# A hybrid attention block on one core: the first attention block prepared inside the last weight tile, and VectorE's sort and mask work in pieces

## The chip, the cores and the metric

One core of one Trainium2 chip. The metric is the device time of one execution in microseconds. The profile is one execution recorded by the hardware profiler; its times are counted from the start of its span.

## The reference

One layer, x of 2048 tokens by 1024, fp32:

```python
proj = x @ w_in                      # qa ka va ga | qi ki wi | qb kb vb gb
# group A: every query keeps the 256 best visible keys, 8 heads, one key/value head
score = sum_h w_h * relu(qi_h . ki)  # visible: key chunk <= query chunk (chunks of 64)
idx   = top_k(score, 256)
ya    = softmax(qa . ka[idx] / 8 - slope * |t - idx|) @ va[idx]
# group B: window of two chunks, 8 heads on 2 key/value heads, a sink per head
yb    = softmax([qb . kb / 8 - slope * dist, sink])[..., :-1] @ vb
y     = concat(ya * silu(ga), yb * silu(gb)) @ w_out
out   = layer_norm(2 ** 0.25 * x + y) * g + b
```

## The kernel before

**The projection.** The weights are 20 tiles of 128 columns, the tokens two halves of 1024. For each half, TensorE takes tile by tile; a `product` is the six matmuls of one of the 8 row blocks k of a tile (`product`, L1345; values are split into a high and a low part, three products each, two banks of 512). ScalarE takes the tile out of the PSUM (`evacuate`) and stores it to `proj` in DRAM. Sixteen groups `norm(b)` of 24 matmuls (L1363) make values and indexer weights in natural layout, into bank 4 or 6; ScalarE takes them out (`leave_norm`).

**The search.** Queries are dealt with in blocks of 128, two blocks to a pair; the pairs come in the order 0, 1, 2, 3, 7, 6, 5, 4, and `p` counts along it (so p = 4 is the longest, with 2048 keys, p = 5 has 1792, p = 6 1536, p = 7 1280). For pair p TensorE makes `dots` (L1377), ScalarE `relu` (L1208), VectorE `sum` (L1580); dots(p, j, c, w, h) is query block j, keys from c, w of them, heads h and h+1, in bank 4 + h for p up to 5. Then VectorE turns the scores into sortable integers (`sortable`, L1596: sign bits, flip, mask to the upper half), and 32 steps of bisection find the level of the 256th key: `search` on VectorE for one block of the pair, `sign` on ScalarE for the other, and for p of 5 and above GpSimd decides (`decide_own`, `decide_sign`). At the end come `limits`, `equal`, and `masks` (L1667): two scans that rank equal keys, one operation that marks those taken, two that write the mask, in one piece.

**The attention.** Blocks b = 0 to 15 follow the same order. For each: the band (`load_qb`, `round_qb`, `split_qb`, `window`, `bias_b`, `exp_b`, `level_b`, `turn_b`, `mix_b`, `gate_b`), the scan for the row maxima (`scan` on TensorE, two banks; `scan_max`, L1733, on VectorE; `turn_max`, `leave_max`, L1757; `place_max`, a DMA), and the units `logits`, `exp_a`, `values` over the key tiles, then `turn_a`, `y_a`, `columns_a`, `gate_a`. From block 12 on, the probabilities are split and `low_a` (VectorE for one half, GpSimd for the other) makes their low part. The scan of block b+1 needs the maximum of block b (L1423). The units of block b need its mask from DRAM for b of 2 and above.

**The hand-over.** Late buffers lie in the memory of early ones. So the first loads wait for the last matmul of the projection: `load_qa(0)`, `load_bias`, `shift_values`, `extra_rows` (constant rows of `qa_ext`, and `upper`), the memsets of `setup_pieces` (L1704, VectorE). `load_keys_a` (L815) puts the raw keys into the buffer of `relu` and waits until the last sum of pair 5 is done; ScalarE rounds them (`round_keys_a`), GpSimd subtracts (`split_keys_a`). The first scan needs all of these.

**The order.** No order is written by hand. `whole_plan` lists pieces with an engine, a cost and what they need; a list scheduler places them, and its ranks are shifted by a table of numbers, `PREFER`, one for each kind of piece. Every engine and DMA queue then runs its pieces in that order.

```python

pe.wait_ge(a_left_max, b)      # scan of block b, L1423
sp.wait_ge(summed, 4 * chunks_before(NPAIR - 2))   # load_keys_a, L817
```

Of the kernel before, what the change touches and what calls it, by code (L numbers as in the profile page):

```python
# [23 lines left out]
F32 = mybir.dt.float32  # L24
# [16 lines left out]
H = 8  # L41
# [31 lines left out]
            "keys_rest", "load_wo")  # L73


def index_chunks(p):


    n = 2 * P * (PAIRS[p] + 1)
    chunks = [(j, c, min(512, n - c)) for j in range(2) for c in range(0, n, 512)]  # L80
    return sorted(chunks, key=lambda chunk: p == NPAIR // 2 and chunk[1] >= HALF)


FAMILY = {"index": ("load_index", "queries", "split_index", "dots", "relu", "sum"),
          "search": ("sortable", "begin", "search", "sign", "turn", "limits", "equal", "above", "masks"),
          "band": ("load_qb", "round_qb", "split_qb", "window", "bias_b", "max_b", "exp_b", "put_sink", "den_b", "level_b", "turn_b",
                   "copy_b", "mix_b", "gate_b"),
          "scan": ("load_qa", "round_qa", "split_qa", "positions", "scan", "scan_max", "top_of_chunks", "turn_max", "leave_max", "place_max"),
          "units": ("logits", "exp_a", "low_a", "values", "leave_a"),
          "tail": ("turn_a", "y_a", "columns_a", "gate_a")}  # L90
# [93 lines left out]
def whole_plan():  # L184
# [6 lines left out]
    def dots_of(p, bank_lock):  # L191
# [5 lines left out]
        for p, j, c, w, h in parts:  # L197
# [7 lines left out]
            add("DVE", 0.25 + 1.05 * w / 512, "sum", *part,  # L205
                needs=[("relu", *part), ("leave_norm", BLOCKS[2 * p + j]), sums[-1], ("masks", p - 1)])
            sums.append(("sum", *part))
        add("DVE", 0.6 + 5.1 * n / 1000, "sortable", p, needs=[sums[-1]])
        add("DVE", 0.15, "begin", p, needs=[("sortable", p), ("store_masks", p - 1)])
        for i in range(32):  # L210
            if i == 16:
# [37 lines left out]
    def products(half, t, k):  # L249
# [1661 lines left out]
```

## Time and profile before

| | us |
|---|---|
| median of 3 runs | 1454.12 (1453.76 to 1454.82) |
| the profiled execution | 1462.23 |
| its span | 1460.4 |
| TensorE busy | 1359.3 (93%) |
| VectorE busy | 1130.6 (77%) |
| ScalarE busy | 896.8 (61%) |
| GpSimd busy | 629.6 (43%) |

The profiled execution is 8.1 us longer than the median. Busy time is that of instructions; register, semaphore and DMA-issuing instructions are not counted. The granted clock of TensorE is given as a share of 2.4 GHz: 1.00, or 0.50 (1.2 GHz), or a mean over a stretch. A row of a timeline has start, duration, engine, line, operation, output <- inputs and, in brackets, the idle time before it with what ended it. Matmuls overlap, so that the distance between two starts is what one costs.

### The profile page before, as it was taken

How to read it: one execution, taken by the hardware profiler on the slowest of the kernel's cores; microseconds unless marked ns; L12 is line 12 of the kernel's file. 1: busy time of each engine (PE TensorE's matmuls, PEld its weight loads, DVE VectorE, ACT ScalarE, POOL GpSimd, SP SyncE). 2: the span in 40 equal slices, each digit the busy share in tenths (PEclk: the TensorE clock that was granted, in tenths of full speed). 3: DMA queues.
4: the chain of work that ended last, by engine and by line, in shares of the span. 5: the costliest groups of instructions: out<-in, count | busy, mean ns of one | idle time of the engine just before them, and what ended most of it. 6: DMA issues, size and time to landing. Idle time of an engine off the chain costs nothing. (4 is left out here: it accounts for less than half of the span.)

```text
span 1460.4 us, 18810 instructions
## 1 busy us (share of the span) xinstructions
PE 1359.3 (93%) x6006; PEld 993.5 (68%) x6052; DVE 1130.6 (77%) x2215; ACT 896.8 (61%) x1687; POOL 629.6 (43%) x726
## 2 busy tenths in 40 slices
PE   7999999899999995798999799999999799999997
PEld 5888887698888874565655456655555565588886
DVE  3486879864899887778889999889898967257675
ACT  3395885873498736777775488885678676700010
POOL 2421332633422336466544256534336577423332
PEclk9999999999999996699999999999999899999999
DMA  7412232325232328233433132402011143134442
GB/s 241 127 60 80 87 105 80 117 91 154 73 109 94 101 90 174 66 89 87 113 92 88 45 83 56 104 21 64 27 28 26 39 133 118 44 122 146 144 148 83
DMA packets 106548, 136.85 MB, mean 94 GB/s; under 512 B 6643, under 2 KB 83383, under 8 KB 106191
## 3 DMA queue, kind: packets, MB, share of 16 engines
q1 hardware_dynamic: 93296, 93.23, 23.4%
q10 hardware_dynamic: 9504, 31.66, 5.5%
q0 software_dynamic: 3648, 10.76, 2.5%
q8 instruction: 48, 0.79, 0.2%
q14 instruction: 52, 0.42, 0.1%
HBM read 92.20 MB, written 42.34 MB: 92 GB/s over the span
## 5 line engine op out<-in xcount | busy, mean ns | idle before, releaser
L1644 DVE TENSOR_SCALAR_CACHE_REDUCE above<-dist,trial 128x512 bf16<-128x512 int32 (+13 forms) x224 | 345.9, 1544 | 28.9 <-POOL trial L1002 23.9
L1179 ACT ACTIVATE above<-dist,trial 128x384 bf16<-128x384 int32 (+13 forms) x224 | 280.8, 1254 | 60.8 <-DVE trial L1617 24.3
L1356 PE MATMUL psum<-x_hi,w_hi 128*128 128x512 f32 x640 | 251.8, 393 | 16.0 <-DVE x_lo L1693 10.6
L1356 PE MATMUL psum<-x_lo,w_hi 128*128 128x512 f32 x640 | 250.8, 392 | 0.0
L1356 PE MATMUL psum<-x_hi,w_lo 128*128 128x512 f32 x640 | 250.5, 391 | 0.0
L1290 ACT ACTIVATE prob<-psum 128x512 f32<-128x512 f32 x272 | 159.8, 593 | 115.8 <-PE psum L1506 54.6
L1748 DVE CUSTOM_DVE_ANT_0 junk<-psum,mask 128x512 bf16<-128x512 f32 (+3 forms) x320 | 184.4, 605 | 26.7 <-PE psum L1430 16.1
L1506 PE MATMUL psum<-prob,vw 128*65 128x512 f32 x376 | 184.8, 597 | 0.1
L1493 PE MATMUL psum<-qa_mix,ka_mix 128*128 128x512 f32 x272 | 162.4, 597 | 5.5 <-DMA qa_ext<-minus_max 3.7
L1430 PE MATMUL psum<-ka_ext,qa_ext 128*128 128x512 f32 (+3 forms) x320 | 134.1, 467 | 27.4 <-ACT ka_mix L1129 12.3
L941 POOL CAST w_hi<-raw 128x1024 fp32r<-128x1024 f32 x40 | 49.7, 1243 | 253.1 <-PE psum L1356 248.8
L1356 PEld LDWEIGHTS psum<-x_hi,w_hi 128*128 128x128 f32 x640 | 121.1, 189 | 43.2 <-issue 11.1
L1356 PEld LDWEIGHTS psum<-x_hi,w_lo 128*128 128x128 f32 x640 | 121.1, 189 | 25.6
L1356 PEld LDWEIGHTS psum<-x_lo,w_hi 128*128 128x128 f32 x640 | 121.2, 189 | 24.9
L1215 ACT ACTIVATE relu<-psum 128x1024 f32<-128x1024 f32 (+1 forms) x76 | 71.4, 957 | 86.2 <-PE psum L1389 54.2
L1593 DVE SCALAR_TENSOR_TENSOR score<-relu,vw,score 128x512 f32<-128x512 f32 (+1 forms) x114 | 101.5, 891 | 12.3 <-ACT relu L1215 5.9
L1494 PE MATMUL psum<-qa_ext,ka_ext 128*128 128x512 f32 x272 | 109.2, 402 | 0.0
L1430 PEld LDWEIGHTS psum<-ka_ext,qa_ext 128*128 128x128 f32 x320 | 63.0, 201 | 66.9 <-issue 32.1
L1129 ACT ACTIVATE yt_hi<-yt_raw 128x1024 fp32r<-128x1024 f32 x16 | 17.0, 1061 | 140.2 <-PE psum L1555 126.7
L949 POOL TENSOR_TENSOR w_lo<-raw,w_hi 128x1024 fp32r<-128x1024 f32 x38 | 100.0, 2632 | 5.8 <-POOL w_hi L941 0.4
L1555 PE MATMUL psum<-wo_hi,yt_hi 128*128 128x512 f32 x256 | 99.8, 390 | 0.1
L1555 PE MATMUL psum<-wo_hi,yt_lo 128*128 128x512 f32 x256 | 99.6, 389 | 0.0
(161 smaller groups left out, 2906.8 us busy)
## 6 DMA issues: line engine op xcount, KB each, us to landing
raw<-w_tiles SPq DMA_DIRECT2D x40, 512.0 KB, 3.7
proj<-staged ACTq DMA_DIRECT2D x40, 512.0 KB, 3.3
qb_raw<-proj SPq DMA_DIRECT2D x32, 256.0 KB, 4.0
qa_raw<-proj SPq DMA_DIRECT2D x32, 256.0 KB, 4.5
yt_raw<-y_t SPq DMA_DIRECT2D x16, 512.0 KB, 5.1
x_row<-x_res SPq DMA_DIRECT2D x16, 512.0 KB, 3.9
out<-z ACTq DMA_DIRECT2D x16, 512.0 KB, 2.6
x_raw<-xT SPq DMA_DIRECT2D x12, 512.0 KB, 4.2
```

What stands on the lines that cost most here:

```text
L949: nc.gpsimd.tensor_tensor(w_lo[:, u, :, :].rearrange("p k c -> p (k c)"), raw[:, u, :], w_hi[:, u, :, :].bitcast(F32).rearrange("p k c -> ...
L1179: nc.scalar.activation(above[:, 0, 0:n], src, ACT.Sign, scale=-1.0, bias=u, accum_out=count[:, 0:1]).then_inc(sign_counted, 1)
L1290: last = nc.scalar.activation(prob[:, unit % 3, :], psum[:, 4 + unit % 2, :], ACT.Exp, scale=0.125)
L1356: last = pe.matmul(psum[:, 2 * u + m, :], wt[:, u, k, :], xt[:, k, 512 * m:512 * m + 512], start=(k == 0 and q == 0), stop=(k == KT - 1 an ...
L1430: last = pe.matmul(psum[:, bank, 0:w], qa_ext[:, s, h, :], ka_ext[:, s, c:c + w], start=True, stop=not diag)
L1493: pe.matmul(o, ka_mix[:, ks], flat(qa_mix[:, s, hs, :]), start=False, stop=False)
L1494: last = pe.matmul(o, ka_ext[:, s, ks], flat(qa_ext[:, s, hs, :]), start=False, stop=(kt < BLOCKS[b]))
L1506: pe.matmul(psum[0:65, 6 + g, :], vw[:, kt, 0:65], prob[:, u % 3, :], start=(kt == 0), stop=(kt == BLOCKS[b])).then_inc(a_used, 1)
L1555: last = pe.matmul(psum[:, 4 + 2 * s + m, :], yt[:, s, k, :], wt[:, k, cols], start=(k == 0 and q == 0), stop=(k == KT - 1 and q == 2))
L1593: v.scalar_tensor_tensor(o, relu[:, h, 0:w], wt, o, ALU.mult, ALU.add).then_inc(summed, 1)
L1644: v.tensor_scalar(above[:, 1, 0:n], src, u, None, ALU.is_ge, ALU.add, accum_out=count[:, 1:2]).then_inc(own_counted, 1)
L1748: v.tensor_tensor_reduce(out=junk[:, scan % 2, 0:w], in0=psum[:, scan % 2, 0:w], in1=mask[:, s, c:c + w], scale=1.0, scalar=-3.0e38, op0=A ...
```

## The change

1. The raw keys go into the memory of `values_hi` and `values_lo` instead of `relu`, so their load no longer waits for the sums of pair 5; `split_values` now waits until the keys are taken.
2. The loads and constants of the first block wait for single products of tile 19 (`last_tile(k)`), not for its end. Buffers are placed anew to allow that: `qa_raw` moves to the front, `yt_a` and `gate_a` behind `y_a`.
3. The memsets of the start leave VectorE (`setup_pieces` is gone) and become seven on GpSimd (`fill`).
4. `sortable` is cut into `sign_bits`, `flip`, `sortable`; `masks` into `rank` (twice), `taken`, `masks`. The operations are the same; other work of VectorE may now stand between the pieces.
5. norm(9) need only stand before tile 19; the plan's costs of `decide_own` and `decide_sign` go from 0.45 to 0.53; the whole of `PREFER` is new, so that many pieces change places.

```diff
+FILLS = 7
-PREFER = {'above': -36689.1, 'band0': -163507.6, ...
+PREFER = {'above': -221597.0, 'band0': -79525.8, ...
-        add("DVE", 0.6 + 5.1 * n / 1000, "sortable", p, needs=[sums[-1]])
+        add("DVE", 0.6 + 1.7 * n / 1000, "sign_bits", p, needs=[sums[-1]])
+        add("DVE", 0.1 + 2.1 * n / 1000, "flip", p, needs=[("sign_bits", p)])
+        add("DVE", 0.1 + 1.3 * n / 1000, "sortable", p, needs=[("flip", p)])
-        add("DVE", 0.9 + n * 0.0077, "masks", p, needs=[("equal", p), ("above", p)])
+        add("DVE", 0.3 + n * 0.0024, "rank", p, 0, needs=[("equal", p), ("above", p)])
+        add("DVE", 0.1 + n * 0.0024, "rank", p, 1, needs=[("rank", p, 0)])
+        add("DVE", 0.2 + n * 0.0022, "taken", p, needs=[("rank", p, 1)])
+        add("DVE", 0.3 + n * 0.0011, "masks", p, needs=[("taken", p)])
...
+        if (half, t) == (1, N_TILES - 1) and k == 0:
+            needs.append(("norm", NORM_ORDER[-1]))
...
-        keys_a_raw = flat(relu)
+        keys_a_raw = [values_hi[:, :, :].bitcast(F32).rearrange("p b n -> p (b n)")[:, 0:HALF],
+                      values_lo[:, :, :].bitcast(F32).rearrange("p b n -> p (b n)")]
+
+        def last_tile(k):
+
+            return (x_used, KT + k) if k < KT - 1 else (tile_mm, 2 * N_TILES)
...
             def load_keys_a():
                 sp.wait_ge(stored[0], 16 * (N_TILES // 2 + 2))
-                sp.wait_ge(summed, 4 * chunks_before(NPAIR - 2))
...
             def load_bias():
-                sp.wait_ge(tile_mm, 2 * N_TILES)
+                sp.wait_ge(*last_tile(1))
...
             def extra_rows():
-                pool.wait_ge(tile_mm, 2 * N_TILES)
+                pool.wait_ge(*last_tile(4))
...
-                settled()
-                nc.gpsimd.memset(row_top[:, :], 0.0).then_inc(setup_pool, 1)
-                latest[0] = (setup_pool, 2)
+            def fill(top):
+
+                pieces = [(2, mask[:, 0, 0:P], 0.0), (2, mask[:, 1, 0:2 * P], 0.0), (2, mask[0:HD, 0, HD:P], -BIG),
+                          (2, mask[0:HD, 1, P + HD:2 * P], -BIG), (2, lb[:, :, 0:HD], 0.0), (5, vs[0:HD, 0, :], 0.0),
+                          (KT - 1, row_top[:, :], 0.0)]
+                for i in ((FILLS - 1,) if top else range(FILLS - 1)):
+                    k, where, value = pieces[i]
+                    pool.wait_ge(*last_tile(k))
+                    settled()
+                    nc.gpsimd.memset(where, value).then_inc(filled, 1)
+                    latest[0] = (filled, i + 1)
...
             def split_values(i):
                 if i == 0:
                     pool.wait_ge(norm_out, NB)
+                    pool.wait_ge(keys_taken, 2)
...
-                if n_dots == 2 * chunks_before(NPAIR - 2):
-                    act.wait_ge(keys_lo, 2)
...
-                elif (half, t) == (0, N_TILES - 1):
+                elif t == N_TILES - 1:
                     last.then_inc(x_used, 1)
...
-                for j in range(2):
-                    last = v.tensor_tensor_scan(rank[:, j, 0:n], equal[:, j, 0:n], equal[:, j, 0:n],
-                                                n_above[:, j:j + 1], ALU.add, ALU.max)
-                step(last)
+                step(v.tensor_tensor_scan(rank[:, j, 0:n], equal[:, j, 0:n], equal[:, j, 0:n],
+                                          n_above[:, j:j + 1], ALU.add, ALU.max))
```

The order on TensorE in tile 18 of the second half. Lines 1356 (before) and 1379 (now) are products, 1387 and 1389 (now 1410 and 1412) dots of pair 5, 1395 norm(9). Before, from dots (5, 0, 512) for heads 2 and 3 on:

```order
L1387 MATMUL psum<-ki_hi,qi_split 128x512
L1389 MATMUL psum<-ki_lo,qi_split 128x512
L1387 MATMUL psum<-ki_hi,qi_split 128x512
L1389 MATMUL psum<-ki_lo,qi_split 128x512
L1356 MATMUL psum<-x_hi,w_hi 128x512
L1356 MATMUL psum<-x_lo,w_hi 128x512
L1356 MATMUL psum<-x_hi,w_lo 128x512
L1356 MATMUL psum<-x_hi,w_hi 128x512
L1356 MATMUL psum<-x_lo,w_hi 128x512
L1356 MATMUL psum<-x_hi,w_lo 128x512
L1387 MATMUL psum<-ki_hi,qi_split 128x512
L1389 MATMUL psum<-ki_lo,qi_split 128x512
```

Now, from the same dots on:

```order
L1410 MATMUL psum<-ki_hi,qi_split 128x512
L1412 MATMUL psum<-ki_lo,qi_split 128x512
L1410 MATMUL psum<-ki_hi,qi_split 128x512
L1412 MATMUL psum<-ki_lo,qi_split 128x512
L1379 MATMUL psum<-x_hi,w_hi 128x512
L1379 MATMUL psum<-x_lo,w_hi 128x512
L1379 MATMUL psum<-x_hi,w_lo 128x512
L1379 MATMUL psum<-x_hi,w_hi 128x512
L1379 MATMUL psum<-x_lo,w_hi 128x512
L1379 MATMUL psum<-x_hi,w_lo 128x512
L1395 MATMUL psum<-wn_hi,x_hi 128x196
L1395 MATMUL psum<-wn_lo,x_hi 128x196
```

The norm, 24 matmuls of which two are shown, moved from the start of the second half to this place. In tile 19 five groups of dots of pair 5 stand now where there were seven, the last two narrow, and the other groups come behind its last product, around the two window groups.

The order on GpSimd around the end of the projection, from the band's first split on. Before:

```order
L1020 TENSOR_TENSOR kb_lo<-kb_raw,kb_hi 128x2x128
L1024 TENSOR_TENSOR qb_mix<-qb_raw,qb_mix 64x2x256 x2
L964 TENSOR_TENSOR qi_split<-qi_raw,qi_split 64x1024
L988 DMA qa_ext<-c_extm 64x1024 x2
L989 DMA upper<-c_upper 128x256
L991 MEMSET row_top 128x128
L981 TENSOR_TENSOR ka_mix<-relu,ka_ext 64x1024
L1067 MEMSET qa_ext 1x1024
```

Now:

```order
L1043 TENSOR_TENSOR kb_lo<-kb_raw,kb_hi 128x2x128
L1047 TENSOR_TENSOR qb_mix<-qb_raw,qb_mix 64x2x256 x2
L1002 DMA qa_ext<-c_extm 64x1024 x2
L1003 DMA upper<-c_upper 128x256
L1014 MEMSET mask 128x128
L1014 MEMSET mask 128x256
L1014 MEMSET mask 64x64 x2
L1014 MEMSET lb 128x8x64
L1014 MEMSET vs 64x128
L1014 MEMSET row_top 128x128
L1091 MEMSET qa_ext 1x1024
L1098 TENSOR_TENSOR qa_mix<-qa_raw,qa_mix 64x1024
```

The split of the indexer's queries for pair 6 moved behind, the splits of the keys stand ahead of this piece, and the fills are new.

The order on VectorE around the masks of pair 5 (p = 5). `minus_max` is `leave_max` of block 7. Before:

```order
L1755 TENSOR_REDUCE row_top<-part_max 128x8
L1761 TENSOR_SCALAR minus_max<-psum 8x128
L1672 TENSOR_SCALAR n_above<-n_above 128x2
L1674 SCALAR_TENSOR_TENSOR score<-score,n_above 128x1792 x2
L1677 SCALAR_TENSOR_TENSOR dist<-score,dist 128x2x1792
L1680 TENSOR_SCALAR above<-dist,trial 128x1792 x2
```

Now:

```order
L1700 SCALAR_TENSOR_TENSOR score<-score,n_above 128x1792
L1822 RECIPROCAL rec_a<-psum 128x8
L1826 TENSOR_TENSOR y_a<-psum,rec_a 128x512
L1769 ISA junk,part_max<-psum,mask 128x512
L1769 ISA part_max 128x1
L1776 TENSOR_REDUCE row_top<-part_max 128x8
L1705 SCALAR_TENSOR_TENSOR dist<-score,dist 128x2x1792
L1808 TENSOR_TENSOR yt_a<-psum,gate_a 128x512
L1711 TENSOR_SCALAR above<-dist,trial 128x1792 x2
L1782 TENSOR_SCALAR minus_max<-psum 8x128
```

The maximum of block 7 stood ahead of the whole mask work and stands behind it now. For pair 5's start, VectorE did all sums, the sort and the first search step ahead of the first band operation; now the last sums and the sort pieces stand between the reductions of blocks 0 and 1, and four search steps come before the second maximum instead of eight. Around the sort of pair 6, sign bits and flip stand ahead of the last reduction of block 8, and y_a of block 7 comes three search steps later instead of right behind the sort. Around the masks of pair 7, `low_a` pieces of block 13 stand ahead of the first scan and between scans and `taken`.

## Rows read from the trace of the kernel before

**Rows 1.** Windows: stretch, its length, busy PE, PEld, DVE, ACT, POOL (instructions), clock, DMA, GB/s
```profile
526.00:536.00 10.00, 7.77 (x29) 6.36 (x30) 7.78 (x13) 4.70 (x5) 0.00 (x0) 0.83 0.47 157
560.00:600.00 40.00, 18.57 (x64) 13.56 (x66) 28.24 (x73) 31.64 (x51) 26.64 (x40) 0.59 0.77 154
760.00:800.00 40.00, 37.16 (x150) 20.83 (x152) 37.23 (x64) 24.61 (x51) 16.95 (x9) 1.00 0.35 88
820.00:850.00 30.00, 17.65 (x75) 12.83 (x75) 29.01 (x64) 17.53 (x35) 11.27 (x22) 0.77 0.25 71
1140.00:1170.00 30.00, 22.56 (x93) 14.76 (x93) 28.62 (x54) 18.59 (x32) 16.03 (x22) 0.78 0.20 58
```

**Rows 2.** Timeline of TensorE, end of the projection: start, duration, what, [idle before]
```profile
555.30 0.39 PE L1356 MATMUL psum<-x_hi,w_lo 128*128 128x512 f32 x1
...
572.14 0.44 PE L1430 MATMUL psum<-ka_ext,qa_ext 128*128 128x128 f32 x1 [12.28 <-ACT ka_mix L1129]
...
584.63 0.99 PE L1493 MATMUL psum<-qa_mix,ka_mix 128*128 128x512 f32 x1 [2.97 <-DMA qa_ext<-minus_max]
```

**Rows 3.** Timelines of SyncE and GpSimd there, and two DMA issues with landing time
```profile
539.37 0.58 SPq L810 DMA_DIRECT2D qb_raw<-proj  x1
...
548.52 2.73 POOL L1024 TENSOR_TENSOR qb_mix<-qb_raw,qb_mix 64x512 fp32r<-64x512 f32 x2
557.54 2.56 POOL L988 DMA_DIRECT2D qa_ext<-c_extm  x2
571.05 0.94 POOL L1067 MEMSET qa_ext<- 1x1024 f32 x1 [3.39 <-DMA upper<-c_upper]
...
power<-c_pow POOLq DMA_DIRECT2D x1, 512.0 KB, 5.1
upper<-c_upper POOLq DMA_DIRECT2D x1, 128.0 KB, 10.9
```

**Rows 4.** Tile 18: timelines of TensorE and ScalarE; and line 1372 in 320 to 420
```profile
520.27 0.39 PE L1387 MATMUL psum<-ki_hi,qi_split 128*128 128x512 f32 x1
522.54 0.39 PE L1387 MATMUL psum<-ki_hi,qi_split 128*128 128x512 f32 x1
528.23 0.47 PE L1387 MATMUL psum<-ki_hi,qi_split 128*128 128x512 f32 x1 [3.27 <-ACT relu L1215]
...
528.74 1.02 ACT L1215 ACTIVATE relu<-psum 128x1024 f32<-128x1024 f32 x1 [0.65 <-DVE score L1593]
...
320.00:420.00 100.00, 7.25 (x65) 7.07 (x64) 1.00 0.39 116
```

**Rows 5.** Timeline of VectorE behind the sums of pair 5
```profile
555.82 3.66 DVE L1607 TENSOR_SCALAR dist<-score 128x3584 int32<-128x3584 int32 x1
559.51 3.89 DVE L1608 TENSOR_TENSOR score<-score,dist 128x3584 int32<-128x3584 int32 x1
563.44 2.03 DVE L1609 TENSOR_SCALAR dist<-score 128x3584 int32<-128x3584 int32 x1
...
566.93 2.08 DVE L1644 TENSOR_SCALAR_CACHE_REDUCE above<-dist,trial 128x1792 bf16<-128x1792 int32 x1
...
581.69 0.28 DVE L1761 TENSOR_SCALAR minus_max<-psum 8x128 fp32r<-8x128 f32 x1 [1.73 <-PE psum L1455]
...
602.27 0.27 DVE L1761 TENSOR_SCALAR minus_max<-psum 8x128 fp32r<-8x128 f32 x1
```

**Rows 6.** Timeline of VectorE, mask work of pair 5
```profile
773.81 4.51 DVE L1677 SCALAR_TENSOR_TENSOR dist<-score,dist 128x3584 f32<-128x3584 int16 x1
778.35 4.13 DVE L1680 TENSOR_SCALAR above<-dist,trial 128x1792 bf16<-128x1792 f32 x2
```

**Rows 7.** Timeline of TensorE behind the sort of pair 6
```profile
832.10 1.09 PE L1531 MATMUL psum<-ident,y_a 128*128 128x128 f32 x4 [6.21 <-DVE y_a L1805]
```

**Rows 8.** Timeline of VectorE, two equal operations of the sums
```profile
539.08 0.49 DVE L1590 TENSOR_SCALAR score<-relu,vw 128x512 f32<-128x512 f32 x1 [0.37 <-ACT relu L1215]
548.64 1.45 DVE L1590 TENSOR_SCALAR score<-relu,vw 128x512 f32<-128x512 f32 x1 [1.22 <-ACT relu L1215]
```

More of the change, by code:

```diff
@@ L84 @@
 FAMILY = {"index": ("load_index", "queries", "split_index", "dots", "relu", "sum"),
-          "search": ("sortable", "begin", "search", "sign", "turn", "limits", "equal", "above", "masks"),
+          "search": ("sign_bits", "flip", "sortable", "rank", "taken", "begin", "search", "sign", "turn", "limits", "equal", "above", "masks"),
           "band": ("load_qb", "round_qb", "split_qb", "window", "bias_b", "max_b", "exp_b", "put_sink", "den_b", "level_b", "turn_b",
@@ L298, in whole_plan @@
             tile(half, t)
-            if (half, t) == (0, N_TILES - 1):
-                for b in NORM_ORDER[0:8]:
+            if t == N_TILES - 1:
+                for b in NORM_ORDER[8 * half:8 * half + 8]:
                     norm(b)
@@ L303, in whole_plan @@
                 products(half, t, k)
-        if half:
-            for b in NORM_ORDER[8:]:
-                norm(b)
         for p in ((1, 2, 3), (4, 5))[half]:
@@ L312, in whole_plan @@
         add("POOL", 1.0, "keys_rest", i, needs=[("norm", NORM_ORDER[-1]), ("split_x2", 2 * KT + 1), ("round_keys", 1)])
[L313 removed]
+    last = lambda k: ("product", 1, N_TILES - 1, k)
+    add("SP", 1.4, "load_keys_a", needs=[("store", 1, 2)])
     for i in range(2):
[L315 removed]
+        add("ACT", 3.2, "round_keys_a", i, needs=[("load_keys_a",), ("split_x2", 2 * KT + 1), ("norm", NORM_ORDER[-1])])
         add("POOL", 2.6, "split_keys_a", i, needs=[("round_keys_a", i)])
     add("POOL", 1.0, "load_power", needs=[("split_w", 1, N_TILES - 1)])
[L318 to L319 removed]
+    add("SP", 0.4, "load_bias", needs=[last(1)])
+    add("POOL", 3.2, "extra_rows", needs=[last(4), ("load_power",)])
     add("ACT", 1.0, "setup_act", needs=[end])
[L321 to L324 removed]
+    for i in range(2):
+        add("POOL", 0.35 if i else 2.2, "fill", i, needs=[end if i else last(5), ("fill", i - 1)])
+    add("ACT", 0.25, "put_sink", 0, needs=[("fill", 0)])
+    add("SP", 3.6, "shift_values", needs=[last(5), ("leave_norm", NORM_ORDER[-1])])
     stores = [("store", 1, N_TILES - 1), ("store", 1, N_TILES - 2)]
@@ L368, in whole_plan @@
         add("SP", 0.4, "place_max", b, needs=[("leave_max", b), ("positions", b)])
-        add("PE", 0.9, "turn_b", b, holds="banks2", until=("copy_b", b), needs=[("level_b", b), ("setup_dve",), ("mix_b", b - 1)])
+        add("PE", 0.9, "turn_b", b, holds="banks2", until=("copy_b", b), needs=[("level_b", b), ("fill", 0), ("mix_b", b - 1)])
         add("ACT", 1.03, "copy_b", b, needs=[("turn_b", b), ("mix_b", b - 1)])
@@ L1741, in scan_max @@
                 if scan == 0:
-                    for i in range(2):
-                        dve.wait_ge(stored[i], 16 * N_TILES)
+                    dve.wait_ge(stored[0], 16 * N_TILES)
+                    dve.wait_ge(tile_mm, 2 * N_TILES)
+                    dve.wait_ge(filled, FILLS)
                 dve.wait_ge(a_scan, scan + 1)
```

113 lines of the change are left out of this document (54 added, 59 removed).

## The prediction

> **What bounds the kernel now.** I read the busy time and the granted clock by stretches first, and of each row the busy time of TensorE, that of VectorE and the clock. From 560 to 600 us, just behind the projection, TensorE is busy 18.57 of 40 us at a mean clock of 0.59, the worst stretch of the kernel. Two smaller dips lie at 820 to 850 (17.65 of 30, clock 0.77) and 1140 to 1170 (22.56 of 30, 0.78), and in both VectorE is full, 29.01 and 28.62 of 30. An ordinary stretch, 760 to 800, has TensorE busy 37.16 and VectorE 37.23 of 40 [rows 1]. So both engines are close to being the bound, and time is lost where TensorE waits for something that the start of the attention or VectorE owes it.
>
> The timeline of TensorE shows the hand-over: the last product starts at 555.30 and ends at 555.7, the first scan comes at 572.14 behind 12.28 us of idle time, the first logits at 584.63 [rows 2]. The queues of GpSimd and SyncE and the landing times show what was late: GpSimd issued the constant rows only from 557.54, because they waited for the end of the projection; the last one, `upper`, took 10.9 us to land and released the memset at 571.05; `power`, on the same queue at a quieter time, took 5.1 [rows 3].
>
> **Step 1: a matmul group that moves.** norm(9), the last of the natural-layout products, goes from the start of the second half into tile 18, behind two groups of dots of pair 5. 65 such matmuls are busy 7.25 us, so its 24 take 2.7 [rows 4], and TensorE reaches tile 18 that much earlier. But norm(9) writes bank 6, which the dots just ahead of it fill. The ReLU that empties the bank ran from 528.74 for 1.02 us, to 529.8, since it waits for sums that stand behind the mask work of pair 4 on VectorE, which does not move. Before, a dots group (4 matmuls) and a product (6 matmuls of the same size) together took 522.54 - 520.27 = 2.27, so 0.91 and 1.36 [rows 4]. Now the two dots groups, and the product between them and norm(9), end at 520.27 - 2.7 + 1.36 + 2 x 0.91 + 1.36 = 522.1. Then TensorE waits until 529.8, 7.7 us where 3.27 stood [rows 4]: **+4.4 us** on the end of the projection. The ends are 0, if VectorE finishes the masks of pair 4 sooner, and +6, if the longer wait doubles the clock loss of the stretch behind it, which was 10 x 0.17 = 1.7 us between 526 and 536 [rows 1].
>
> **Step 2: the hand-over.** From 529.8, norm 2.7, two dots groups 1.8, four products 5.4 and the clock loss of 1.7 end tile 18 at 541.4. Tile 19 has eight products (10.9) and now 3.7 of dots, so the projection ends at 556.0; another 3.7 us of dots that used to lie inside it come behind. The band's loads are issued at the end of tile 18. Before, they were issued from 539.37, and GpSimd's split of the queries ended at 548.52 + 2.73 = 551.25, 11.9 later [rows 3]; that gives 553.3 now. The constant rows come right behind it. Their issue took 2.56 plus 0.6 for `upper`, so they are out at 556.4, and `upper` lands between 561 (with 5.1) and 567 (with 10.9). The fills that left VectorE run on GpSimd meanwhile. VectorE had 1.46 us for them and `begin` between 563.44 + 2.03 and 566.93 [rows 5]; on GpSimd the flight of `upper` covers them, and without that cover I would charge 2. The keys' six copies on ScalarE, 1.02 each by the ReLU of the same size [rows 4], lie in tiles 18 and 19, beside dots which VectorE paces.
>
> VectorE is late by its own account. Of pair 5, the sums of (1,512) and (1,1024) and the eight band operations now stand ahead of its first reduction, and each dots group needs its ReLU and sums before a buffer is free. Behind 556.0 come a dots group, a ReLU (1.02), and two and a half double groups of sums at 4 x 0.5 to 4 x 0.9, which with about 2 of band work reach 566 to 567. I take the first scan at **567, 5 us earlier** than 572.14; the ends are 562 (all as early as the quick landing allows) and 572 (nothing gained).
>
> From there to the first maximum (`leave_max`) it took 9.6 us, 572.14 to 581.69, with a search step of 2.08 inside. That span now also holds 2.0 of sums (four at 0.49 [rows 8]), 3.66 of sign bits and 3.89 of flipping [rows 5], and no search step: 9.6 if these fall into VectorE's waits, 17 if all waits stay. With 12.5 the maximum comes at 579.5 and the logits 2 us earlier than before. Up to the second maximum VectorE owes 2.03 of sorting, four search steps and eight reductions; that is 595 instead of 602.27, with four steps (8.3 us) fewer done [rows 5]. TensorE is 7 us ahead and VectorE's total work 1 behind. As neither engine alone is the bound [rows 1], I take **-3 us, step 1 included**, between -7 and +1.
>
> A rule speaks against giving GpSimd more to do. An operation that takes VectorE 0.49 at 539.08 took 1.45 at 548.64 [rows 8], beside GpSimd's subtraction that began at 548.52 [rows 3]. I keep to that excess, 1 us for each of three subtractions that run beside sums and sort pieces, and the -3 holds it. The Trainium skill (SBUF — State Buffer, "Who interferes with whom") makes it a lock: a VectorE operation with two SBUF inputs or in a two-port mode and a GpSimd one that reads SBUF exclude each other for a whole instruction. By that rule the trace agrees; what it would do here in full is the third rival.
>
> **Step 3: the parts.** Cutting adds one semaphore wait between the two scans of a pair; I cost it at nothing, against scans of several us. What counts is what now stands between the pieces.
> - Pair 6, at 820 to 850. TensorE waits 6.21 us for y_a, which stands behind the whole sort [rows 7]; it is idle 12.4 in all [rows 1]. Now four key tiles of block 7 stand beside sign bits and flip, and only the last sort piece, a search step and gate_b stand before the maximum: -5.
> - Pair 7, at 1140 to 1170, 7.4 idle [rows 1]. Low halves of block 13 now stand between mask pieces, but the two scans stay together: -3.
> - Pair 5, the other way round. Before, the maximum of block 7 came ahead of the mask work, and TensorE ran block 7 beside it, busy 37.16 of 40 from 760 to 800 [rows 1]. Now `taken` (4.51) and `masks` (4.13) [rows 6] and gate_a (about 0.7) stand ahead of that maximum, and TensorE's next work, the scan of block 8, needs it: 9.3 us idle. The units it would have done are not lost; they fill its holes up to 850. I charge 5.
>
> Sum of step 3: **-3 us**, between -9 and +6.
>
> **Sum.** -3 - 3 = -6 us. The profiled execution took 1462.23 us with a span of 1460.4, 8.1 above the median of the runs; the terms are differences inside it, so I take them from the median, 1454.1: **1448 us**.
>
> **Rivals.**
>
> *The maximum behind the masks (slower).* If block 7's units find no hole later, all 9.3 us stay, and the clock falls as it did at 820 to 850: 30 x 0.23 = 7 us of clock there for 12.4 of idle time, so 5 for 9.3. With +1 for the hand-over and -8 for the other two places that is +7: 1461; with -3 for the hand-over 1457. I put 1459. It decides when more than 8 us of the wait and its clock stay. For it: no such wait exists there now. Against: VectorE is full behind it, so TensorE has holes anyway. Chance 0.21.
>
> *VectorE is the bound (no change).* The search of pair 5 starts four steps late, each pair starts when the one before is done, and TensorE's 7 us become idle time before the masks. The same comes out if `upper` lands late and the change does not bring the first scan forward. +1 for the hand-over and -1 for the parts: 1454. For it: VectorE is busy 28.24 of 40 in the gap itself, so there is not much to win for it. Chance 0.15.
>
> *GpSimd's reads stop VectorE.* Three subtractions of 2.73 [rows 3] delay VectorE by 8.2 instead of the 3 in the sum, so -6 becomes -1: 1453. One operation in the rows was held for 1 us, none for 2.7. Chance 0.07.
>
> *Both gains in full.* TensorE's 7 us carry to the end and the parts give back 8: 1439. For it: TensorE is 93% busy there, so a lead counts. Chance 0.17.
>
> **How the numbers follow.** The forecast has 0.40, with a range of its own from 1444 to 1451. About 0.2%, 2.9 us, is what a measurement of this kernel can tell from no change. The forecast counts as faster but for 0.02, the full gain wholly, the first rival as slower, the second and third as the same but for 0.05, split. That makes faster 0.58, same 0.19, slower 0.23. The range from 1438 to 1460 leaves out the far ends of the full gain and of the slower rival.
>
> **What would show it.** After the change: a wait of TensorE of 7 to 8 us before norm(9) in tile 18 (step 1); the first scan at 566 to 568 and the second maximum near 595, with four search steps before it instead of eight (step 2); an idle stretch of some 9 us before the first scan of block 8, released by `minus_max`, and clearly less than 12.4 us idle around the sort of pair 6 (step 3). I am wrong if the first scan comes after 570, if no idle time stands at the masks of pair 5, or if the end of the attention moves the other way than the sum.

## The result, and the profile after

| | before | after |
|---|---|---|
| median | 1453.94 (1452.88 to 1454.82, 4 runs) | 1469.03 (1466.26 to 1469.82, 4 runs) |
| the profiled execution | 1462.23 | 1468.81 |
| VectorE busy | 1130.6 | 1142.6 |

Times in us. The ratio is 1.0101, with a 95% interval from 1.0083 to 1.0118: **15 us slower**, outside the range forecast. The two profiled executions lie only 6.6 us apart, because that of before is 8 us above its median and that of after is not. Whether what was read in [rows 1] belonged to that one execution is a question for the first experiment.

The same stretches as in [rows 1], after the change:

```profile
526.00:536.00 10.00, 10.00 (x43) 8.71 (x43) 0.00 (x0) 6.98 (x9) 5.86 (x4) 0.79 0.46 105
560.00:600.00 40.00, 24.10 (x95) 18.11 (x96) 34.54 (x82) 25.05 (x42) 29.86 (x33) 0.64 0.42 98
760.00:800.00 40.00, 28.90 (x118) 19.03 (x118) 36.30 (x75) 16.18 (x28) 9.33 (x8) 0.79 0.20 62
820.00:850.00 30.00, 25.47 (x113) 15.55 (x113) 28.01 (x61) 22.46 (x32) 12.71 (x32) 1.00 0.30 89
1140.00:1170.00 30.00, 23.33 (x99) 14.17 (x101) 27.81 (x31) 23.47 (x47) 25.01 (x25) 0.94 0.18 53
```

The three bad stretches of before are better (24.10 of 40, 25.47 of 30, 23.33 of 30), and the good one, 760 to 800, is now bad: TensorE is busy 28.90 at a clock of 0.79. The timeline of TensorE shows the places that the prediction named:

```profile
523.50 0.50 PE L1395 MATMUL psum<-wn_hi,x_hi 128*128 128x196 f32 x1 [4.66 <-ACT relu L1237]
...
559.84 0.30 PE L1453 MATMUL psum<-ka_ext,qa_ext 128*128 128x128 f32 x1 [0.77 <-POOL qa_ext L1091]
...
576.10 0.80 PE L1410 MATMUL psum<-ki_hi,qi_split 128*128 128x512 f32 x1 [5.62 <-POOL qi_split L978]
...
774.44 0.76 PE L1453 MATMUL psum<-ka_ext,qa_ext 128*128 128x512 f32 x1 [8.28 <-DVE minus_max L1782]
```

norm(9) waits 4.66 us. The first scan starts at 559.84, 12.3 earlier than in [rows 2]. Right behind the first maximum TensorE waits 5.62 us for GpSimd's split of the queries of pair 6. The scan of block 8 waits 8.28 us for the maximum of block 7. VectorE, at that maximum, against [rows 6], and at its first two maxima, against [rows 5]:

```profile
573.88 0.28 DVE L1782 TENSOR_SCALAR minus_max<-psum 8x128 fp32r<-8x128 f32 x1
579.49 2.08 DVE L1672 TENSOR_SCALAR_CACHE_REDUCE above<-dist,trial 128x1792 bf16<-128x1792 int32 x1
...
593.63 0.27 DVE L1782 TENSOR_SCALAR minus_max<-psum 8x128 fp32r<-8x128 f32 x1
...
765.49 5.52 DVE L1705 SCALAR_TENSOR_TENSOR dist<-score,dist 128x3584 f32<-128x3584 int16 x1
771.66 2.34 DVE L1711 TENSOR_SCALAR above<-dist,trial 128x1792 bf16<-128x1792 f32 x2
773.92 0.27 DVE L1782 TENSOR_SCALAR minus_max<-psum 8x128 fp32r<-8x128 f32 x1
```

The first maximum comes 7.8 us earlier, the second 8.6 earlier, with four search steps between sort and second maximum. So the hand-over did more than was forecast, the wait at the masks of pair 5 is there with nearly its forecast length, the dip at the sort of pair 6 is gone, and yet the kernel is 15 us slower.

### The profile page after: what moved, and what is told of

Read it like the earlier page. It is cut to its first block, busy times and chain, and to the rows that moved or that the text cites. A ratio compares the mean times of both kernels' runs of the same rounds, so it can differ in the third digit from the quotient of the medians.

```text
span 1467.0 us, 18822 instructions
## 1 busy us (share of the span) xinstructions
PE 1359.0 (93%) x6005; PEld 993.0 (68%) x6052; DVE 1142.6 (78%) x2209; ACT 897.9 (61%) x1687; POOL 634.5 (43%) x732
## 4 chain that ended last, share of the span: by engine, by line
PE 58%; DVE 14%; ACT 13%; issue 6%; POOL 6%; DMA 2%; SPq 1%; ACTq 0%; POOLq 0%; DVEq 0%
PE psum L1578 11%; PE psum L1529 10%; PE psum L1379 8%; ACT above L1203 7%; PE psum L1453 4%; PE psum L1516 4%; PE psum L1517 3%; DVE above L1672 3%; PE psum L1515 3%; PE psum L1395 3%; ACT accept L1211 2%; PE psum L1410 2%; ACT trial L1214 2%; DVE score L1616 1%; PE psum L1412 1%
## 5 line engine op out<-in xcount | busy, mean ns | idle before, releaser
L1453 PE MATMUL psum<-ka_ext,qa_ext 128*128 128x512 f32 (+3 forms) x320 | 139.9, 480 | 32.2 <-DVE minus_max L1782 14.1
L1616 DVE SCALAR_TENSOR_TENSOR score<-relu,vw,score 128x512 f32<-128x512 f32 (+1 forms) x114 | 97.2, 853 | 12.5 <-ACT relu L1237 5.2
```

The costliest lines, as they stand in the source:

```text
L1453: last = pe.matmul(psum[:, bank, 0:w], qa_ext[:, s, h, :], ka_ext[:, s, c:c + w], start=True, stop=not diag)
L1616: v.scalar_tensor_tensor(o, relu[:, h, 0:w], wt, o, ALU.mult, ALU.add).then_inc(summed, 1)
```

## The experiments

All experiments but the two that replace a subtraction leave the operations of the changed kernel as they are and give the engines another order. The list of pieces is written out in place of the plan's own:

```diff
-    order = planned_order()
+    order = given_order()
```

Of each, the edit to that list is shown. `up_to(a, piece, b)` stands for list a as far as the piece, and then all that is left, in the order of b; `old` is the order of before (with the new pieces in it), `new` that of the change. In e6 and e16 a few pieces of bands 14 and 15 stand further back than this rule puts them, since block 12 holds the PSUM bank that they need. Medians are compared by the ratio to runs of before on the same chip (their medians were 1454.5 to 1456.1); a thousandth is 1.45 us.

### Code and order apart

```diff
+    order = old                                   # e1
+    order = up_to(new, ("limits", 5), old)        # e2
+    order = up_to(old, ("limits", 5), new)        # e3
```

> The changed code (hand-over, fills on GpSimd, keys in the values' memory, costs) with the order of before: sort and mask pieces contiguous, every piece of every engine where it stood before; only the fills follow the constant rows and the splits of the values follow the first split of the queries, as the new waits ask. Theory A (the maximum of block 7 behind the masks costs what the hand-over gained; order, not code, made the 15 us): near 1450 to 1454, first scan some 1 to 3 us earlier than 572, no 8 us wait at the masks of pair 5. Theory B (the code itself costs, by work moved to GpSimd or by later splits of the values): 1460 or more.

> The order of the changed kernel up to the limits of pair 5 (about 745 us), the order of before for all that is left. The trace gives the changed kernel a lead of some 12 us there. Theory A: the lead stays but for the holes it fills, 1442 to 1448. Theory C (the tail is bound by VectorE's searches, so a lead is used up by waits whatever the order): 1452 to 1456. Theory D (the loss lies in the front, before 745, and the trace's lead is only work that was put off): above 1460.

> The reverse: the order of before up to the limits of pair 5, the new order behind it, with the maximum of block 7 behind the masks. Theory A: about 13 us of wait and clock at the masks of pair 5, 12 back around the sort of pair 6, 13 lost in small pieces between 880 and 1240: 1465 to 1470. Theory C: 1454 to 1458, since the order of the tail does not matter. Theory D: at or below 1454.

| | median | ratio, 95% interval |
|---|---|---|
| e1, old order | 1457.01 | 1.0012 (1.0003 to 1.0022) |
| e2, new to 745 us, then old | 1454.66 | 0.9991 (0.9981 to 1.0001) |
| e3, old to 745 us, then new | 1472.59 | 1.0115 (1.0100 to 1.0130) |
| the change, all new | 1469.03 | 1.0101 (1.0083 to 1.0118) |

The code with the old order costs 1.7 us by the ratio, more than theory A's 1450 to 1454 and far less than theory B's 1460. The new order of the front gains 3.0 us (e1 to e2) or 2.0 (e3 to the change). The new order behind 745 us costs 16.0 (e2 to the change) or 15.0 (e1 to e3). Theory D, a loss in the front, falls. Of theory A, order and not code makes the loss, as it said, but the lead of the front was not kept: e2 lies in theory C's 1452 to 1456. Theory C was right that the lead is used up in the old tail, and wrong in "whatever the order", for which e3 should have come at 1454 to 1458. e2 is the best version that computes everything, and it cannot be told from before.

The profile of e1 also settles the first question. In the old order the first scan still starts at 572.38:

```profile
572.38 0.45 PE L1796 MATMUL psum<-ka_ext,qa_ext 128*128 128x128 f32 x1 [14.48 <-ACT ka_mix L1496]
```

So it is the order that brings the first scan forward, not the code alone. For TensorE the stretch of the gap itself is in e1 nearly as it was before (18.57 of 40, clock 0.59):

```profile
560.00:600.00 40.00, 19.40 (x63) 13.19 (x63) 23.15 (x63) 29.64 (x49) 30.08 (x40) 0.59 0.71 141
```

The two stretches behind it, of before and then of e1 (L1796 is its scan):

```profile
600.00:640.00 40.00, 34.57 (x133) 25.53 (x135) 31.19 (x75) 24.85 (x46) 19.93 (x38) 0.70 0.32 75
640.00:720.00 80.00, 72.73 (x326) 46.53 (x331) 63.17 (x185) 63.45 (x136) 46.98 (x77) 0.96 0.36 88
```

```profile
600.00:640.00 40.00, 32.72 (x151) 22.84 (x152) 35.04 (x82) 29.39 (x53) 21.85 (x45) 0.85 0.32 75
640.00:720.00 80.00, 72.78 (x346) 46.88 (x345) 66.53 (x195) 66.10 (x144) 51.65 (x79) 1.00 0.39 97
```

Busy time by granted clock gives TensorE's work: 34.57 x 0.70 + 72.73 x 0.96 = 94.0 for before, 32.72 x 0.85 + 72.78 x 1.00 = 100.6 for e1. That is 6.6 of the 8 us by which the profiled execution of before is longer than its median, mostly as a low clock. They lie behind the rows from which the hand-over was priced: the first two maxima come at 581.69 and 602.27 in that execution, and at 582.30 and 604.28 in e1.

The traces of e1 and e2 show what became of the lead. The first maximum of e2 comes at 573.04, 9.3 us ahead of e1's; its maximum of block 7 comes at 757.90, ahead of e1's (758.65) by 0.8. VectorE starts the search of pair 5 at 578.65 in e2 and at 563.67 in e1, so the lead of TensorE runs into a search that is late, as the second rival of the prediction had it. That this is what ate the lead is read from the traces; no run isolates it.

### The wait at the masks of pair 5

```diff
 top_of_chunks 7                       # e4, VectorE
+leave_max 7
 taken 5
 gate_a 6
 masks 5
-leave_max 7
```

> The changed kernel with one operation of VectorE moved: the maximum of block 7 stands ahead of taken of pair 5, not behind gate_a and the masks. Theory A: the wait of 8.28 us before the scan of block 8 goes, and with it the low clock of 770 to 780; of 13 us lost there 6 to 12 come back: 1457 to 1463. If the tail as a whole is what costs (C or B), 1466 to 1470, the time of the changed kernel, with the idle time turning up later.

1466.28, ratio 1.0071 (1.0056 to 1.0086): 2.7 us less than the change by the medians and 4.4 by the ratios. Less came back than the 6 to 12 forecast; the time is in the range of the other theory, and the idle time did turn up again: TensorE waits 4.02 us for `yt_a` and then 3.55 for a `part_max`, both behind the mask work.

```diff
-rank 5 0, rank 5 1, taken 5, masks 5  # e9, VectorE: from between the reductions
 leave_max 7
+rank 5 0, rank 5 1, taken 5, masks 5
```

> The changed kernel with both ranks, taken and masks of pair 5 in one row behind the maximum of block 7, as before; only VectorE's order changes, and only there. Theory H (the wait at the masks of pair 5 is not the maximum alone: by then TensorE has nothing in store that does not come through VectorE, so only mask work that starts behind the maximum lets it run): the 13 us of wait and clock shrink to 3 to 6, 1459 to 1464, more than the 2.7 that the maximum alone gave back. Rival (mask work of 16 us in one row starves the sums of pair 6 and the scan of block 8 as much): 1465 to 1470.

1474.59, ratio 1.0139 (1.0122 to 1.0156): 5.5 us slower than the change, and slower than both theories had it. Theory H falls in this form, since the wait nearly doubled:

```profile
783.54 1.30 PE L1796 MATMUL psum<-ka_ext,qa_ext 128*128 128x512 f32 x2 [15.34 <-DVE part_max L2112]
```

In the old list, mostly logits and values of blocks 6 and 7 stand behind `turn_max 7` on TensorE, which need nothing more from VectorE. In the new list it is scans of block 8 and dots of pair 6, whose banks come free only through VectorE, with a few logits of block 7 between them. That this is what makes VectorE's long row dear here is read from the lists; no run changed TensorE's list at this place.

### The sort of pair 6 and the masks of pair 7

```diff
 sign_bits 6                           # e8, VectorE, from e2
+y_a 7
 flip 6
 sortable 6
-y_a 7
```

> The run cut at pair 5 (new front, old tail, 1454.7) with one operation moved on VectorE: y_a of block 7 between the sign bits and the flip of pair 6, instead of behind the sort. There TensorE waits 6.21 us for it at 824.7, at a low clock behind. Theory G (the pieces are worth what the prediction said): the wait falls to about 1 us, 1448 to 1452. Rival (TensorE's next work hangs on VectorE's maxima anyway, so the wait moves behind the sort): 1453 to 1456.

1457.10, ratio 1.0014 (1.0004 to 1.0025): 3.3 us slower than e2 by the ratio, 2.4 by the medians. The wait of e2 is the first row, that of e8 the second:

```profile
824.69 1.09 PE L1897 MATMUL psum<-ident,y_a 128*128 128x128 f32 x4 [6.21 <-DVE y_a L2169]
```

```profile
827.57 0.69 PE L1796 MATMUL psum<-ka_ext,qa_ext 128*128 128x384 f32 x1 [7.09 <-DVE part_max L2112]
```

The wait moved to the next thing that needs VectorE, as the rival said, though the time is 1 us above its range. Putting this one result between the pieces of the sort gains nothing.

```diff
-low_a 13 0, low_a 13 1, low_a 13 2    # e7, VectorE: from ahead of and between the pieces
 masks 7
+low_a 13 0, low_a 13 1, low_a 13 2
```

> The changed kernel with three low_a operations of VectorE (block 13, key tiles 0 to 2) behind the masks of pair 7 instead of ahead of and between the pieces; nothing else moves. Theory E: the operations of VectorE and GpSimd that hold each other up there (7.62 us for two subtractions of GpSimd that take 1.29 each elsewhere, VectorE's low parts at 1.5 to 2.1 instead of 0.69) part, masks 7 end 3 to 5 us earlier: 1463 to 1467. Rival F (the low parts are needed at once by TensorE, which then waits for them behind the whole mask work, as the cut was meant to avoid): 1469 to 1473.

1472.04, ratio 1.0123 (1.0105 to 1.0142), 3.2 slower than the change by the ratio: in the range of rival F. The two intervals overlap, so that the pieces do what they were cut for at this place is likely, not shown.

### The two engines that hold each other up

VectorE and GpSimd around the masks of pair 7, after the change:

```profile
1156.45 2.12 DVE L1814 TENSOR_TENSOR prob_lo<-prob,prob_hi 128x512 fp32r<-128x512 f32 x1
1158.82 6.62 DVE L1700 TENSOR_TENSOR_SCAN score<-score,n_above 128x1280 int16<-128x1280 bf16 x2
```

```profile
1158.89 7.62 POOL L1077 TENSOR_TENSOR prob_lo<-prob,prob_hi 128x512 fp32r<-128x512 f32 x2
```

Before, the median of VectorE's low parts is 0.69 us and that of GpSimd's 1.29. Here one of VectorE takes 2.12, and two of GpSimd take 7.62 beside two scans of 6.62. Two runs replace GpSimd's subtraction by a memset, which leaves the low part of that half out:

```diff
-                nc.gpsimd.tensor_tensor(prob_lo[:, u % 3, :], prob[:, u % 3, :],
-                                        prob_hi[:, u % 3, :].bitcast(F32), ALU.subtract).then_inc(a_low[0], 1)
+                nc.gpsimd.memset(prob_lo[:, u % 3, :].bitcast(F32), 0.0).then_inc(a_low[0], 1)
```

> The changed kernel (1469) with GpSimd's subtraction for the low half of the probabilities (46 of them, block 12 on) replaced by a memset of zeros of the same tile: it leaves out the low part of one half of the probabilities from block 12 on, and GpSimd reads nothing there. Theory E (the two engines hold each other up): VectorE's low parts fall back to 0.69 us, its excess of 11 us behind 1120 against the old order goes, and this kernel gains more than the same edit does in the old order: 1458 to 1463. Rival (the order itself leaves TensorE without work there): 1465 to 1469.

> The same memset in the old order with the changed code (1457.0). It too leaves out the low part of one half of the probabilities from block 12 on. Theory E: 1453 to 1456, so that the distance between the two orders falls from 12 to 5 or 8. Rival: the distance stays at 12.

1459.98, ratio 1.0033 (1.0022 to 1.0044), in the new order; 1448.16, ratio 0.9956 (0.9941 to 0.9970), in the old. The edit gains 9.9 us in the one and 8.1 in the other. The distance between the orders was 12.9 and is 11.2: theory E, which I had formed from those rows, explains some 2 us of the loss, with an uncertainty as large. That the subtraction is what holds VectorE up is shown at the same place of e11, where the low part and the two scans are back at 0.68 and 5.80:

```profile
1158.30 0.68 DVE L2156 TENSOR_TENSOR prob_lo<-prob,prob_hi 128x512 fp32r<-128x512 f32 x1
1159.10 5.80 DVE L2042 TENSOR_TENSOR_SCAN score<-score,n_above 128x1280 int16<-128x1280 bf16 x2
```

The subtraction is dear in both orders.

### Where in the tail

The first two cuts:

```diff
+    order = up_to(new, ("limits", 6), old)        # e5
+    order = up_to(new, ("limits", 7), old)        # e6
```

> The new order up to the limits of pair 6 (about 965 us), the old order behind it. The stretch between the two cuts (745 to 965) holds the maximum of block 7 behind the masks, the sort of pair 6 in pieces and blocks 8 to 10. Theory E (the 8.3 us wait at the masks of pair 5 is mostly given back around the sort of pair 6, and the loss comes later, where low_a and the mask work meet GpSimd): 1457 to 1460, so 2 to 5 above the run cut at pair 5 (1454.7). Theory A (that wait and what follows it make the loss): 1463 to 1468.

> The new order up to the limits of pair 7 (about 1150 us), the old order for the masks of pair 7 and the last two blocks. Theory E (loss where low_a stands beside and between the mask pieces, behind 1150): 1459 to 1463. If the loss lies in the steps of pair 7 between 965 and 1150 (blocks 11 to 13): 1466 to 1470.

1475.02 (1.0141) and 1475.47 (1.0146), both slower than the whole new order, which no theory had. Where two orders are joined, the pieces that one has done and the other has not make a seam, and the seam has a price of its own. By the plan's costs the orders differ by 32 and 15 us at these two points. In e5 TensorE waits 7.39 us there for a tile of the band, in e6 11.39 us for a `prob_lo` of block 13 that now stands behind the masks of pair 7. These two runs say nothing on the place of the loss. Together with e2, the next four cut at about 745, 830, 895 and 1150 us, where the orders differ by 5, 8, 15 and 9 us.

```diff
+    order = up_to(new, ("scan_max", 9, 0, 512), old)                                        # e13
+    order = up_to(new, ("limits", 5), up_to(old, ("search", 6, 1), new))                    # e14
+    order = up_to(new, ("search", 6, 18), old)                                              # e15
+    order = up_to(new, ("logits", 13, 0, 1), old)                                           # e16
```

> New order to about 830 us (behind the sort of pair 6), old order behind. Beside the run cut at 745 (1454.7) it adds the masks of pair 5 and the sort of pair 6 in the new order. Theory J (that stretch takes 13 us at the masks and gives back 12 at the sort, a net of 1 to 3): 1455 to 1458. Theory A (it is the place of the loss): 1464 to 1469.

> The changed kernel (1469) with the old order only from 745 to 830 us. Theory J: 1466 to 1469, since what the wait at the masks costs is what the pieces of the sort give back. Theory A: 1455 to 1458.

> New order to about 895 us, old order behind. Theory J with the loss spread over the late stretches: 1456 to 1460. If the loss lies in blocks 8 and 9 beside search 6: 1464 or more.

> New order to about 1150 us, old order for the masks of pair 7 and the last two blocks. Where the profile of the changed kernel loses 7 us against the old tail between 1160 and 1200 and 2.6 behind it: 1459 to 1462. If the loss lies between 895 and 1150 (a wait for round_qa ahead of an exponential at 913, the masks of pair 6, the maximum of block 12): 1466 to 1470.

| new order up to | median | ratio | step in us |
|---|---|---|---|
| nowhere (e1) | 1457.01 | 1.0012 | |
| 745 (e2) | 1454.66 | 0.9991 | -3.0 |
| 830 (e13) | 1460.07 | 1.0029 (1.0016 to 1.0041) | +5.5 |
| 895 (e15) | 1462.41 | 1.0031 (1.0015 to 1.0047) | +0.3 |
| 1150 (e16) | 1467.55 | 1.0070 (1.0050 to 1.0090) | +5.7 |
| the end (the change) | 1469.03 | 1.0101 (1.0083 to 1.0118) | +4.5 |

By the medians the last four steps are +5.4, +2.3, +5.1 and +1.5. Only the step to 830 and that to 1150 lie between intervals that do not overlap, and each step holds the price of a seam: e6 and e16 leave the new order within eight pieces of each other, and their medians lie 8 us apart. e13 and e15 came between the ranges of their two theories; e16 lies in the range for a loss between 895 and 1150, which its seam makes uncertain. So the loss has no single place, but how large it is in each of these stretches is not shown. Even the first step doesn't stand by itself: e14, the change with the old order from 745 to 830, is at 1469.45 (1.0085, 1.0065 to 1.0106), which cannot be told from the change. TensorE is busy there as before, and what it gained is lost behind. Windows of e14:

```profile
760.00:800.00 40.00, 37.42 (x150) 21.25 (x149) 39.58 (x71) 22.42 (x44) 15.19 (x8) 1.00 0.30 80
820.00:850.00 30.00, 20.93 (x82) 15.23 (x82) 26.38 (x53) 13.82 (x20) 9.59 (x26) 0.77 0.25 70
```

The same five stretches of e2, and then of the change:

```profile
745.00:830.00 85.00, 73.41 (x287) 43.20 (x285) 80.55 (x158) 47.30 (x90) 28.03 (x19) 0.96 0.27 71
830.00:895.00 65.00, 60.36 (x272) 38.57 (x273) 60.52 (x168) 54.48 (x122) 35.18 (x79) 0.97 0.26 67
895.00:1040.00 145.00, 141.78 (x581) 82.52 (x580) 130.50 (x291) 103.75 (x205) 61.68 (x105) 1.00 0.20 53
1040.00:1150.00 110.00, 104.12 (x422) 60.62 (x421) 95.37 (x190) 85.19 (x141) 59.56 (x137) 0.96 0.13 36
1150.00:1290.00 140.00, 131.54 (x598) 86.09 (x597) 78.33 (x172) 85.09 (x157) 82.72 (x54) 0.98 0.29 90
```

```profile
745.00:830.00 85.00, 72.56 (x272) 43.33 (x274) 78.12 (x160) 46.11 (x88) 21.34 (x19) 0.90 0.21 58
830.00:895.00 65.00, 61.76 (x273) 39.03 (x279) 57.70 (x154) 55.01 (x121) 34.48 (x75) 1.00 0.26 65
895.00:1040.00 145.00, 137.28 (x542) 79.28 (x551) 123.32 (x277) 93.62 (x179) 54.53 (x94) 0.98 0.22 57
1040.00:1150.00 110.00, 104.77 (x420) 60.83 (x427) 96.03 (x202) 90.24 (x162) 58.65 (x146) 0.98 0.14 37
1150.00:1290.00 140.00, 124.66 (x549) 79.29 (x557) 91.79 (x172) 90.42 (x166) 94.04 (x58) 0.97 0.26 83
```

Busy time by clock, the change less e2 (72.56 x 0.90 - 73.41 x 0.96 = -5.2 for the first): -5.2, +3.2, -7.2, +2.7, -8.0, together -14.5 us of TensorE's work, against 14.4 between the medians. That the two agree is partly luck: over the same stretches the sum is -12.8 for e13 and -21.6 for e16, which are 5.4 and 12.9 us slower than e2. The rows tell where TensorE did less, not what it cost. The first holds the masks of pair 5 and the sort of pair 6. The third has no term in the prediction, and the fifth holds the masks of pair 7 and much behind them.

When VectorE reaches the same piece of work in the two orders is a second measure. The masks of pair 6, in the change and in e2:

```profile
983.54 2.84 DVE L1711 TENSOR_SCALAR above<-dist,trial 128x1536 bf16<-128x1536 f32 x2
983.76 3.87 DVE L2054 TENSOR_SCALAR above<-dist,trial 128x1536 bf16<-128x1536 f32 x2
```

The change is done with the masks of pair 6 at 986.4, 1.2 us ahead of e2, and comes to the scans for those of pair 7 at 1158.82, 12.0 behind it (1146.85). By this mark most of the 14.3 us between the two executions has shown by then. One thing that stands in this stretch, in the timelines of SyncE and then of VectorE of the change:

```profile
984.65 0.60 SPq L823 DMA_DIRECT2D qb_raw<-proj  x1
...
987.36 0.54 SPq L870 DMA_DIRECT2D mask<-masks  x1
```

```profile
992.34 0.69 DVE L1769 CUSTOM_DVE_ANT_0 junk<-psum,mask 128x512 bf16<-128x512 f32 x1 [3.80 <-DMA mask<-masks]
```

The new list puts the band's four loads of block 15 ahead of the mask of block 11 on SyncE, and the sums of pair 7 behind that block's first reduction on VectorE. VectorE, the engine the pair waits for, stands still for 3.80 us, and the search of pair 7 starts at 1037.07 where e2 has 1029.54. In e2 the mask's load is issued at 983.33, and VectorE never waits for one. That wait was not taken away in a run; it is read from the trace alone, and what it costs is open.

### Single waits

```diff
-round_qa 10                           # e17, ScalarE
 exp_a 9 1 0
+round_qa 10
```

> The changed kernel (1469) with one exchange on ScalarE: the rounding of the queries of block 10 (two copies, 2.1 us, which wait for the last values of block 8) behind the first exponential of key tile 1 of block 9 instead of ahead of it. TensorE waits 2.64 us for that exponential at 913.65, and the clock falls behind it; the old order has no such wait. If such waits are the loss one by one: 1465 to 1467. If TensorE then meets the next wait (its holes come from VectorE's pace): 1468 to 1470.

1469.07, ratio 1.0096 (1.0081 to 1.0110): no difference from the change, as the second theory had it. The wait of 2.64 us for the exponential is gone, but one of 2.56 us for `out_a` stands in its place, at 913.72.

```diff
 turn_max 0                            # e18, TensorE, from e2
-dots 6 0 0 512 0
 scan 1 0 0
 scan 1 1 0
+dots 6 0 0 512 0
```

> The run with the new front and the old tail (1454.7) with the first dots of pair 6 behind the first two scans of block 1 on TensorE, which had waited 5.63 us in front of them for GpSimd's split. Theory I: 1451 to 1453.5, since block 1's scan, and with it VectorE's maxima, starts 2 to 3 us earlier. Rival (VectorE, with the sort and the sums of pair 5 still to do, is full there): 1454 to 1456.

1455.30, ratio 0.9998 (0.9986 to 1.0010), not to be told from e2: the rival.

```diff
 split_qa 0                            # e10, GpSimd, from e2
+split_index 6
 split_qb 1
 positions 1
-split_index 6
```

> The run with the new front and the old tail (1454.7), with GpSimd's split of the indexer's queries of pair 6 moved ahead of the band's second split. The dots of pair 6 wait 5.63 us for it at 575, and the split itself took 5.58 there. Theory I (the early first scan bought 2.4 us instead of 12 because other first needs, this one first of all, came late): the wait goes, 1450 to 1453. Rival (VectorE is the bound from there to the end of search 5, as my second rival had it, so nothing that feeds TensorE earlier helps): 1454 to 1457.

1463.24, ratio 1.0057 (1.0042 to 1.0072), 9.6 us slower than e2 by the ratio and 8.6 by the medians, which neither theory had. The positions of block 1, a DMA of GpSimd, now stand behind the split, and the scan of block 1 waits for them:

```profile
581.33 0.55 PE L1796 MATMUL psum<-ka_ext,qa_ext 128*128 128x256 f32 x1 [8.56 <-DMA ka_ext<-c_pos]
```

## Why the prediction was wrong

**Step 1** (+4.4 for the wait of norm(9)): the mechanism was right, the size wrong. The wait is 4.66 us, not 7.7, so 1.4 more than the 3.27 that stood there, and the projection ends at 551.5 instead of 556.0. The sentence that failed is that the mask work of pair 4 "does not move". It ends 6.4 us earlier: the ReLU behind it is over at 522.33 + 1.02 = 523.4, not 529.8, as VectorE's searches start earlier from the first pairs on (that of pair 4 at 391.57 instead of 398.59).

**Step 2** (-3, step 1 included): right in the sum, by the cuts -3.0 or -2.0. The parts were not: the first scan is 12.3 us earlier, not 5; the second maximum comes at 593.63, near the 595 forecast. The rest of that lead is gone by the maximum of block 7 (9.3 us become 0.8, e2 against e1). The 5.62 us for `qi_split` are not what ate it: e18 shows that putting other work ahead of this wait gains nothing, and e10 that serving it first costs more elsewhere. That the sum was right with parts that were not is partly luck.

**Step 3** (-3): this is the step that failed. It took three places, +5, -5 and -3, for the whole effect of the new order behind 745 us; the runs measured +15 to +16 for it (e1 to e3, e2 to the change). For pair 5 the idle time of 8.28 us stands where 9.3 was forecast. For pair 6 the 6.21 us are gone. I had charged +5 and -5; the cut at 830 measured +5.5 for both together, and in the surroundings of the new order nothing that can be told (e14). The -3 for pair 7 may have the right sign for the pieces themselves (e7), but the new order from 1150 on measured +4.5 by the ratios and +1.5 by the medians, no gain. And the stretch from 895 to 1150, where VectorE falls from 1.2 us ahead of e2 to 12.0 behind by 1159, had no term at all. I had read the order at the three places that the cut pieces touch and taken the rest as unchanged, though the change replaces the whole table that makes the order. The costs of such a change can't be summed over a few places: every queue must be gone through, SyncE's too.

**The rivals.** *The maximum behind the masks* (1459, 0.21) had the right sign and the right wait, but not the size: moving the maximum gave 2.7 to 4.4 us back (e4), restoring the stretch nothing that can be told (e14). *VectorE is the bound* names what became of the lead in the front, and the pattern of the single moves: e8, e17 and e18 each took a wait away, and the time stayed or rose. It was wrong in "no change", since VectorE itself can be made to wait, as it is for the mask of block 11. *GpSimd's reads stop VectorE*: true as a mechanism, as e11 shows; but both orders pay it nearly alike. The Trainium skill (SBUF — State Buffer, "Who interferes with whom") has the later of the two wait for a whole instruction. The trace agrees: the slowest of GpSimd's subtractions takes 3.87 us where the median is 1.29, so 2.6 more, and a scan over 1280 elements takes 2.9 undisturbed (e11).

What stays open is how the 10 us behind 895 divide among single waits. Two orders were compared there, the one wait that was moved (e17) gave nothing, and the wait for the mask of block 11 was not touched.

## What to carry to other kernels

When a change replaces what sets the order of a whole program, cut the program in time, give the front one order and the rest the other. Three such runs (e1 to e3) showed here that the whole loss comes from the new order behind 745 us. Cut where both have done nearly the same work, and mistrust small steps even so, since two seams at nearly the same place differed by 8 us here. In this kernel no single wait of the busiest engine was worth its length when it was taken away (waits of 2.6 to 8.3 us, between 3.3 lost and 4.4 gained): ask what stands next in the waiting engine's list, and whether that too comes through the late one. And a long row on one engine can be covered by what stands beside it in the other's list, so the two have to be read together, with the queue that loads for both.

## What the runs showed of the hardware

GpSimd's subtraction for the low part and VectorE's operations delay each other, by more than their own length: 7.62 us for two that take 1.29 each elsewhere, while VectorE's went from 0.69 to 2.12 (0.68 at the same place in e11). GpSimd's split of the queries took 5.57 us beside VectorE's sort, where the median of the seven such splits is 2.39. With all 42 of GpSimd's subtractions for the low part (the expectation above miscounted them as 46) replaced by memsets, the kernel ran 8 to 10 us faster in either order. With the old order that is the only time measured here that can be told from before as faster, and it leaves work out.
